# A hybrid decoder trunk on one core: the first two column groups of layer 0 interleaved, chunks of x turned later, and four edits beside it

## The reference, cut to what matters

```
for l in range(DEPTH):
    h = rms_norm(x, attn_norm_w[l])
    proj = h @ w_in[l]
    q, k, v, z, xbc, dt_raw = split(proj)
    attn = sliding_window_attention(q, k, v, ...)
    ssm  = mamba2_mixer(z, xbc, dt_raw, ...)   # conv of width 4 over tokens, SiLU, scan, gate
    x = x + concat([attn, ssm]) @ w_out[l]
    h = rms_norm(x, ffn_norm_w[l])
    x = x + (silu(h @ w_gate[l]) * (h @ w_up[l])) @ w_down[l]
```

## Time and profile before

| | us |
|---|---|
| median of 3 runs (lowest, highest) | 2099.28 (2098.88, 2099.76) |
| the profiled execution: its own time | 2099.08 |
| its span, first to last instruction | 2097.3 |

### The profile page before, as it was taken

The page is one execution under the profiler, slowest core; times in us unless marked ns, Lnnn a source line. Parts: engine busy times, 40 slices in busy tenths (PEclk is TensorE's granted clock), DMA queues, the critical chain, the costliest instruction groups (busy, mean ns, idle before and its releaser), DMA issues.

```text
span 2097.3 us, 38625 instructions
## 1 busy us (share of the span) xinstructions
PE 2088.9 (100%) x16799; PEld 1988.6 (95%) x16799; DVE 1360.1 (65%) x1571; ACT 1018.6 (49%) x1263; POOL 182.0 (9%) x236
## 2 busy tenths in 40 slices
PE   9999999999999999999999999999999999999999
PEld 8987899999999999999999878999999999998887
DVE  6887866555555555555568878665555555568888
ACT  5555744444444444444435557454444444445454
POOL 1034200000000000000000432000010001100000
PEclk9999999999999999999999999999999999999999
DMA  7674466666666666666656644666667666678785
GB/s 225 183 215 149 128 200 195 191 193 196 194 192 194 197 193 192 192 191 199 192 172 191 209 142 139 196 189 192 205 206 212 203 206 205 202 222 258 242 263 188
DMA packets 209993, 411.95 MB, mean 196 GB/s; under 512 B 13008, under 2 KB 13408, under 8 KB 209824
## 3 DMA queue, kind: packets, MB, share of 16 engines
q1 hardware_dynamic: 202752, 390.24, 61.5%
q0 software_dynamic: 7040, 19.24, 3.1%
q10 hardware_dynamic: 32, 0.01, 0.0%
HBM read 402.06 MB, written 7.37 MB: 195 GB/s over the span
## 4 chain that ended last, share of the span: by engine, by line
PE 98%; ACT 1%; DMA 0%; DVE 0%; issue 0%; ACTq 0%
PE ps L871 73%; PE ps L626 11%; PE ps L649 7%; PE ps L665 1%; PE ps L664 1%; PE ps L666 1%; PE ps L708 1%; PE ps L850 1%; PE ps L828 0%; PE ps L827 0%; PE ps L803 0%; DMA xr<-in_x_dram 0%; ACT stage L1115 0%; DMA raw<-in_w_in_dram 0%; PE ps L788 0%
## 5 line engine op out<-in xcount | busy, mean ns | idle before, releaser
L1351 DVE TENSOR_TENSOR w_lo_s<-raw,w_hi_s 128x1024 fp32r<-128x1024 f32 x549 | 678.6, 1237 | 598.9 <-ACT w_hi_s L1067 597.8
L1067 ACT CAST w_hi_s<-raw 128x1024 fp32r<-128x1024 f32 x549 | 576.2, 1050 | 770.2 <-PE ps L871 756.9
L871 PE MATMUL ps<-h_hi,w_hi_s 128*128 128x256 f32 x3192 | 885.3, 277 | 1.1 <-DVE h_lo L1431 0.6
L871 PE MATMUL ps<-h_hi,w_lo_s 128*128 128x256 f32 x3192 | 883.6, 277 | 0.0
L871 PE MATMUL ps<-h_lo,w_hi_s 128*128 128x256 f32 x3192 | 883.5, 277 | 0.0
L871 PEld LDWEIGHTS ps<-h_hi,w_hi_s 128*128 128x128 f32 x3192 | 599.7, 188 | 1.7 <-DVE h_lo L1431 0.8
L871 PEld LDWEIGHTS ps<-h_hi,w_lo_s 128*128 128x128 f32 x3192 | 600.0, 188 | 0.0
L871 PEld LDWEIGHTS ps<-h_lo,w_hi_s 128*128 128x128 f32 x3192 | 599.9, 188 | 0.0
L871 PE MATMUL ps<-f_hi,w_hi_s 128*128 128x256 f32 x1192 | 330.9, 278 | 0.0
L871 PE MATMUL ps<-f_hi,w_lo_s 128*128 128x256 f32 x1192 | 330.1, 277 | 0.0
L871 PE MATMUL ps<-f_lo,w_hi_s 128*128 128x256 f32 x1192 | 330.1, 277 | 0.0
(11 more groups left out here) (271 smaller groups left out, 2018.1 us busy)
## 6 DMA issues: line engine op xcount, KB each, us to landing
raw<-in_w_gate_dram SPq DMA_DIRECT2D x176, 512.0 KB, 3.8
raw<-in_w_up_dram SPq DMA_DIRECT2D x176, 512.0 KB, 4.2
raw<-in_w_down_dram SPq DMA_DIRECT2D x176, 512.0 KB, 4.3
raw<-in_w_in_dram SPq DMA_DIRECT2D x144, 512.0 KB, 3.6
raw<-in_w_out_dram SPq DMA_DIRECT2D x64, 512.0 KB, 4.2
h_lo<-s_kept POOLq DMA_DIRECT2D x18, 512.0 KB, 4.8
cum_all<-cum_kept POOLq DMA_DIRECT2D x8, 512.0 KB, 5.1
s_kept<-vtok POOLq DMA_DIRECT2D x10, 256.0 KB, 3.7
```

What stands on the lines that cost most here:

```text
L871: done = nc.tensor.matmul(ps[:, bank + m // 2, m % 2 * TOK:(m % 2 + 1) * TOK], w[:, slot, k, m * P:(m + 1) * P], h[:, rows + k, :], start= ...
L1067: nc.scalar.copy(split_buffers(pair)[0][:, slot, :, :], raw[:, slot, :, :]).then_inc(hi_split, 1)
L1351: v_.tensor_tensor(lo[:, slot, :, :], raw[:, slot, :, :], hi[:, slot, :, :].bitcast(F32), ALU.subtract).then_inc(lo_split, 1)
```

## The change

Six edits go together, all but two in layer 0.

- Order of the first two groups: (g, q) = (0,0), (0,1), (1,0), (1,1), then (0,2) to (0,7), then (1,2) to (1,7), as pairs 0 to 15. Ring slots go by p. Group 0 ends at pair 9, group 1 at pair 15.
- Chunks of x: loads behind pairs 1, 2 and 3; `turn_x` 1, 2, 3 behind pairs 1, 3 and 5; `first_hi` and `first_lo` at p = 2, 4, 6; `x_square` at 0, 1, 5, 6; `keep_x` at 2, 3, 7, 8; `first_sum` at 8 instead of 6.
- Banks of the chunks 4, 6, 4, 6: `turn_x(2)` waits for `keep_x(0)`, `turn_x(3)` for `keep_x(1)`.
- Follow-up in layer 0: `turn_vecs` behind pair 9, `dt_products` and `spread_rs` behind 10, `channels(0)` and `conv` at 11 to 14, `silu(0)` at 15; `dt_in`, the exponential, `softplus` and `conv_out(0)` stay at 13, 14, 15 and 16.
- The credits come from two memsets on DVE, POOL's four memsets go; WARM is 8.
- `FURTHER_ON` has pairs 3 and 11 too, in both layers.

```diff
-WARM = 5
+WARM = 8
@@
+    FIRST = [(0, 0), (0, 1), (1, 0), (1, 1)] + [(g, q) for g in range(2) for q in range(2, PPG)]
+
+    def place(layer, p):
+        return FIRST[p] if layer == 0 and p < 2 * PPG else (p // PPG, p % PPG)
+
+    def used_by(layer, g):
+        return layer * PAIRS + (FIRST.index((0, PPG - 1)) + 1 if layer == 0 and g == 0 else (g + 1) * PPG) + RING
@@
-        FURTHER_ON = (7, 15, 19, 27, P_OUT + 7, ...
+        FURTHER_ON = (3, 7, 11, 15, 19, 27, P_OUT + 7, ...
@@
         def x_bank(n):
-            return (4, 6, 2, 4)[n]
+            return (4, 6, 4, 6)[n]
@@ SP
-                    w, r, col = w_in, 2 * (p % PPG), IN_COLS[p // PPG]
+                    g, q = place(layer, p)
+                    w, r, col = w_in, 2 * q, IN_COLS[g]
...
-                    if layer == 0 and p in (1, 3, 4):
-                        load_x(sp, (1, 3, 4).index(p) + 1)
+                    if layer == 0 and p in (1, 2, 3):
+                        load_x(sp, p)
@@ POOL
-            for s, credit in ((lo_split, RING), (pair_used, RING)):
-                pool.memset(numbers[:, 5:6], 0.0).then_inc(s, credit)
-                once(pool.memset(numbers[:, 6:7], 0.0))
@@ PE
-                if n == 3:
-                    pe.wait_ge(x_kept, 1)
+                if n > 1:
+                    pe.wait_ge(x_kept, n - 1)
...
+                for p in range(G_IN * PPG):
+                    g, q = place(layer, p)
...
+                    if (g == 0 or layer == 0 and g == 1) and base + p:
+                        pe.wait_ge(h_lo_ready, layer * 16 + (q + 1))
...
-                        if layer == 0 and p in (0, 2, 4):
-                            turn_x(1 + p // 2)
+                    if layer == 0 and p in (1, 3, 5):
+                        turn_x((p + 1) // 2)
...
-                        if layer == 0 and p == 6:
-                            pe.wait_ge(h_lo_ready, 8)
-                            pe.wait_ge(x_kept, 2)
-                            turn_vecs(layer)
-                        if layer == 0 and p == 7:
-                            pe.wait_ge(x_kept, 3)
+                    if layer == 0 and p == 9:
+                        pe.wait_ge(h_lo_ready, 8)
+                        pe.wait_ge(x_kept, 4)
+                        turn_vecs(layer)
...
-                        if p == 8:
+                    if p == (8 if layer else 10):
@@ ACT
             split(1)
-            first_hi(1, (0,))
             split(2)
-            first_hi(1, (1,))
...
-                    if layer == 0 and p in (2, 4):
-                        first_hi(1 + p // 2)
+                    if layer == 0 and p in (2, 4, 6):
+                        first_hi(p // 2)
...
-                    if layer == 0 and p in (0, 1, 4, 5):
-                        x_square((0, 1, 4, 5).index(p))
+                    if layer == 0 and p in (0, 1, 5, 6):
+                        x_square((0, 1, 5, 6).index(p))
...
-                    if 13 <= p < 38 and p % 8 == 5:
+                    if p == (13 if layer else 15) or 21 <= p < 38 and p % 8 == 5:
                         silu(layer, p // 8 - 1)
@@ DVE
+            v_.memset(numbers[:, 5:6], 0.0).then_inc(lo_split, RING)
+            v_.memset(numbers[:, 6:7], 0.0).then_inc(pair_used, RING)
...
-                    if layer == 0 and p in (2, 3, 6, 7):
-                        keep_x((2, 3, 6, 7).index(p))
+                    if layer == 0 and p in (2, 3, 7, 8):
+                        keep_x((2, 3, 7, 8).index(p))
+                    if layer == 0 and p == 8:
+                        first_sum()
...
-                    if 9 <= p < 37 and p % 8 in (1, 2, 3, 4):
+                    if (9 <= p < 13 if layer else 11 <= p < 15):
+                        conv(layer, 0, p - (9 if layer else 11))
+                    if 17 <= p < 37 and p % 8 in (1, 2, 3, 4):
                         conv(layer, p // 8 - 1, p % 8 - 1)
```

More of the change, by code:

```diff
@@ new lines, in _ @@
+                for p in range(G_IN * PPG):
+                    g, q = place(layer, p)
+                    if q == 0:
+                        if g >= 6:
+                            pe.wait_ge(act_evac, layer * 5 + (g - 5))
+                        elif g >= 2:
+                            pe.wait_ge(ch_ready, layer * 4 + (g - 1))
+                        elif layer:
+                            pe.wait_ge(down_added, layer * DCH - 1 + g)
+                        if 6 <= g:
+                            pe.wait_ge(qk_sums, layer * 3 + (g - 5))
+                    if (g == 0 or layer == 0 and g == 1) and base + p:
+                        pe.wait_ge(h_lo_ready, layer * 16 + (q + 1))
+                    if base + p == 0:
+                        first_products(in_bank(layer, g))
+                    elif g < 4:
+                        products_turned(p % RING, base + p, 2 * q, in_bank(layer, g), q == 0, q == PPG - 1)
+                    else:
+                        products(p % RING, base + p, 2 * q, in_bank(layer, g), h_hi, h_lo, q == 0, q == PPG - 1)
+                    if layer == 0 and p in (1, 3, 5):
+                        turn_x((p + 1) // 2)
+                    if layer and p == 5:
+                        x_total(layer, 0)
+                    if layer == 0 and p == 9:
+                        pe.wait_ge(h_lo_ready, 8)
+                        pe.wait_ge(x_kept, 4)
+                        turn_vecs(layer)
+                    if p == 12:
+                        turn_dt(layer)
+                    if p == (8 if layer else 10):
+                        pe.wait_ge(vec_ready, layer + 1)
+                        dt_products(layer)
+                        spread_rs(layer, 0)
+                    if p in CONV_TURNS:
+                        conv_out(layer, CONV_TURNS.index(p))
+                    if p == CONV_TURNS[1]:
+                        cumulate(layer)
+                    if p == CONV_TURNS[2]:
+                        turn_cum(layer)
+                    if p == 39:
+                        c_times_b(layer)
+                    if p in KQ_TURNS:
+                        turn_qk(layer, KQ_TURNS.index(p))
+                    if p in SCAN:
+                        scan(layer, SCAN.index(p))
+                    if p in TURN_P:
+                        turn_p(layer, TURN_P.index(p))
+                    if p in WEIGH:
+                        weigh_v(layer, WEIGH.index(p))
+                    if 56 <= p and p % 2 == 0:
+                        scores(layer, (p - 56) // 2)
+                    if p == 61:
+                        turn_qk(layer, 2)
@@ L1537, in channels @@
                     dve.wait_ge(rsb_ready, layer * 2 + 1)
-                dve.wait_ge(pair_used, layer * PAIRS + ((j + 1) * PPG + RING))
+                dve.wait_ge(pair_used, used_by(layer, j))
                 at = in_bank(layer, j)
@@ L1703, in _ @@
             split_lo(1)
-            first_lo(1, (0,))
             split_lo(2)
-            first_lo(1, (1,))
             for layer in range(DEPTH):
@@ L1717, in _ @@
                         score(layer, (p - 56) // 2)
-                    if layer == 0 and p in (2, 4):
-                        first_lo(1 + p // 2)
+                    if layer == 0 and p in (2, 4, 6):
+                        first_lo(p // 2)
                     if p - 1 in SCAN:
@@ L1746, in _ @@
                         softplus(layer)
-                    if p == 9 or 15 <= p < 32 and p % 8 == 7:
-                        channels(layer, p // 8 - 1 if p == 9 else p // 8)
-                    if 9 <= p < 37 and p % 8 in (1, 2, 3, 4):
+                    if p == (9 if layer else 11) or 15 <= p < 32 and p % 8 == 7:
+                        channels(layer, p // 8 if p % 8 == 7 else 0)
+                    if (9 <= p < 13 if layer else 11 <= p < 15):
+                        conv(layer, 0, p - (9 if layer else 11))
+                    if 17 <= p < 37 and p % 8 in (1, 2, 3, 4):
                         conv(layer, p // 8 - 1, p % 8 - 1)
```

56 lines of the change are left out of this document (3 added, 53 removed).

## The result

| | before | after |
|---|---|---|
| median, us (lowest to highest) | 2099.39 (2098.88 to 2099.91), 6 runs | 2106.42 (2106.21 to 2107.17), 6 runs |
| profiled execution: its own time | 2099.08 | 2106.21 |
| its span | 2097.3 | 2104.5 |

The kernel became 7.0 us slower: ratio 1.0034, 95% interval 1.0025 to 1.0044. Forecast was 2104.1 within 2101.6 to 2107.3. One run of one later kernel (2608.53 us, at a mean granted clock of 0.752) stood in a slower state and is left out of its numbers.

A forecast was written before the change was run, and what follows sets the result against it. It took TensorE's own queue to bound the kernel (busy 2088.9 of 2097.3 us), paced early by the waits from 17 to 26 us. Terms 4.1 + 0.9 - 0.2 = +4.8 us gave 2104.1, range 2101.6 to 2107.3.

The forecast's parts named there:

- a wait of about 5 us: On PE at turn_x(2), for DVE's keep_x(0): about 5 us of waiting where there was 0.29.
- The chain of 7.20 us from the landing: Early layer 0: from pair 4's landing through ACT and DVE to the waiting turn takes 7.20 us, as before the change.
- The stalls before pairs 4 and 8: PE waits in early layer 0: both go; the one before pair 8 gives 0.73 us, the other is swallowed.
- The forecast's own case: Whole kernel: 2104.1 us, own range 2103.0 to 2105.5, at full clock behind the wait; chance 0.42.
- the rival with the clock: Behind the wait at turn_x(2): PE's clock falls in the gap, +2.2 us, giving 2106.3; chance 0.33.
- The landing: Pair 4's load, now ninth instead of eighth: lands at 19.68, 1.3 us later; bounds 0 and 2.2.
- As before: Rival on pair 4's load: it lands as before, the chain is 1.3 us shorter, time 2102.8; chance 0.13.
- Convolution: Ahead of conv_out(0) in layer 0: PE newly stalls 0.87 us for SiLU; bounds 0 and 1.6.
- Further buffers: Pairs 3 and 11, both layers, in further buffers: -0.2 us in all; bounds -1.2 and +0.5.
- Nothing on the path: Kernel start, credits on DVE and eight warm-up products: no effect on the time; bounds -0.1 and +0.1 us.
- The stretch from the turn to pair 16: PE in layer 0, from turn_x(2) to pair 16: 37.87 us, against 35.06 from turn_x(3) before.

The follow-up runs named there:

- the kernel with the late dt work: The changed kernel with dt_in at iteration 15 and the exponential and softplus at 16 in layer 0: 2105.47 us, ratio to before 1.003.

## Why the prediction was right, and where it was not

**Right: direction, place and mechanism.** `turn_x(2)` waits for `keep_x(0)`, which hangs on the landing of pair 4 by a fixed chain. Forecast: a wait of about 5 us that ends at 26.88; measured 5.70, at 27.27. Taking it away took the whole loss away. The chain of 7.20 us from the landing held within 0.05 in six kernels of seven. The stalls before pairs 4 and 8 went as counted.

**How near the number came is in part luck.** The forecast's own case ended at 2105.5; 2106.42 lies in the range only because the range took in the rival with the clock. That rival's 2106.3 fits so well because its errors cancel: its clock was 0.5 us too dear, its landing 0.4 us too early.

**The landing was 0.4 us under.** Read off by its place in the queue it was to be 19.68, and came at 20.11. As a law this step is worse than its number: the loads as before gave 16.98 where the eighth place had been 18.37. POOL's small loads alone moved it by 4.0 us when they were held back, and kernels with the same loads differ by 0.9 from profile to profile. "As before" was a rival at 2102.8; the kernel with the old loads came to 2103.37, but with the clock fallen and a landing 1.4 us before the old one, so the nearness is chance.

**The clock: the term that the forecast's own case left out.** The forecast took full speed behind the gap and gave the fall 0.33; the fall is what happened. The granted clock went to 0.50 within 5.70 us without work, and filling the gap kept it at 1.00. Measured 1.72 us (0.77 in the turn, 0.95 in pair 4) against the rival's 2.2: it had taken the 4.5 us of the start, here PE worked at the low level for 3.4, and for 5.4 in the kernel with the late dt work (26.34 to 31.73). The rule of the Trainium skill (TensorE: Matmul & The Clock Gate, section Why this matters for your kernels), that idle gaps of some microseconds between bursts put the clock back, agrees with these traces: idle 3.96, 4.87 and 5.70 us, the clock fell; 1.51 and 1.86 us, it didn't. With the fall in the sum, 2104.1 + 1.7 would have been 2105.8, and with the landing 2106.2. The argument against it, that PE had worked right up to the gap, was worth nothing.

**Convolution.** Forecast 0.87 of stall; measured 0.66 of wait, and 0.70 came back with the edit undone. The stretch from pair 16 to 24 lost 1.10; the other 0.4 lies in slower pairs, and what makes a stretch slow was not settled.

**Further buffers.** -0.2 forecast, +0.26 measured alone, and +0.23 behind pair 24 in the kernel after. Both are within what the runs can tell from nothing. Alone, the pairs named changed as forecast; the forecast had left out that later stretches change too and take it back.

**"Nothing on the path" for the start was wrong** for the kernel before, where credits and warm-up are worth 1.3 us. Part of it is the earlier landing of pair 4, which the forecast left out when it read the landings off the kernel before, and part comes with the longer warm-up. In the kernel after this gain can't be seen: its ninth load landed 0.4 later than the ninth before, not earlier.

The stretch from the turn to pair 16 was forecast at 37.87. Measured 39.23, less 1.72 for the clock is 37.51; the count of work moved was right within 0.4 us.

## What to carry to other kernels

When a buffer is shared that was not shared before, look up where the copy that frees it stands in its engine's queue, and what load that queue is waiting for: the price is that landing plus the chain, minus the moment when the waiting engine gets there. Where that leaves TensorE idle for as long as here (3.96 us was enough in most runs, 1.86 in none; nothing between was tried), add half of the time that it then works at the lower level (1.7 us for 3.4 here), and where the wait can't go, fill it with products. Landing times read off a queue's order hold to about a microsecond, and only as long as nothing moves in the other queues.

## What the runs showed of the hardware

- Small loads cost bandwidth far beyond their bytes: from 11 to 15.97 us 232 GB/s with POOL's parameter loads among the big ones, 407 without, at a DMA share of 0.94 and 1.05. Pair 4 landed 4.0 us sooner without them.
- A longer wait doesn't by itself cost more clock. The clock fell 2.29, 3.43 and 4.44 us after PE's last product (idle for 5.70, 4.87 and 3.96), the last time when PE was already back at work, and stayed low for 6.83, 6.83 and 3.41 us. What counts is how much of that PE works through: 3.42, 5.39 and 3.41 us. Behind 3.96 us turn and pair 4 together took 5.27 us, against 0.82 + 2.72 at full clock.
- In one kernel, changed only in the buffers of pairs 3 and 11, the first eight products took longer, though nothing there was changed (before, at 8.34, they took 1.19):

```profile
8.63 1.95 PE L699 MATMUL ps<-h_hi,w_hi_s 128*128 128x256 f32 x8
```

Eight products in 1.95 us are as wide apart as those behind the wait at the lower level, yet the clock column of these windows of PE reads 1.00, as it also does over the slow warm-up of the earlier trace rows. The reason lies in the trace: its record of the clock begins with the rise to full, at 10.33 us here and at 6.57 in the kernel before, and ahead of the first entry the views print 1.00. The spacing changes at these two moments, so it was the clock. At the start go by the spacing, not by the column:

```profile
8.00:9.00 1.00, 1.00 (x7) 1.00 1.04 395
9.00:10.00 1.00, 1.00 (x6) 1.00 1.03 397
```

When the fast spacing begins varies, with a start that is the same, by 3.8 us between these two profiles, and 0.5 us of difference in a single profile may be that.
